# Layout of the norms' roots across partitions: matmuls become transposes, and stand a quarter of a tile earlier in three stages

## The reference

```python
for i in range(2):                      # fox mixer, then nsa mixer
    x = x + mixer_i(rmsnorm(x, norm_g[i]))
x = rmsnorm(x, final_g)
for layer in range(2):                  # hgrn mixer, then mla mixer
    x = x + mixer(_rmsnorm(x, norm_mix[layer]))
    x = x + _conv_ffn(_rmsnorm(x, norm_ffn[layer]), ...)
def _rmsnorm(x, gain):
    return x * rsqrt(mean(x * x, axis=-1) + 1e-6) * gain
def _hgrn2_mixer(h, w_in, lower_bound, out_norm, w_out):
    q, f, i, g = split(h @ w_in, 4)
    forget = lb + (1.0 - lb) * sigmoid(f)
    o = _chunk_gated_recurrence(silu(q), 1 - forget, i, log(forget))
    return (_rmsnorm(o, out_norm) * silu(g)) @ w_out   # norm per head of 128
def _conv_ffn(h, w_up, conv_w, conv_b, w_down):
    gate, up = split(causal_conv3(h @ w_up), 2)        # 2 x 2816
    return (silu(gate) * up) @ w_down
```

## Time and profile before

| | |
|---|---|
| median of 3 runs | 1025.72 us (1021.55, 1025.72, 1028.17) |
| the profiled execution | 1021.83 us |
| its span, first to last instruction | 1020.0 us |
| PE (matmul) busy | 986.8 us, 8176 records |
| DVE busy | 767.8 us |
| ACT busy | 549.8 us |
| POOL busy | 65.8 us |
| mean granted clock of TensorE | 0.996 of full speed |

### The profile page before, as it was taken

How to read it: one execution, slowest core, us unless ns; L and a number is a source line. 1 busy time by engine, 2 the same in 40 slices (tenths; PEclk the granted TensorE clock), 3 DMA queues, 4 the chain that set the end, 5 groups by cost and what they waited for, 6 DMA issues and landing times. The chain is left out here.

```text
span 1020.0 us, 20361 instructions
## 1 busy us (share of the span) xinstructions
PE 986.8 (97%) x8176; PEld 938.1 (92%) x8178; DVE 767.8 (75%) x1300; ACT 549.8 (54%) x869; POOL 65.8 (6%) x54
## 2 busy tenths in 40 slices
PE   7999999999999999999999999999999999999997
PEld 5999999897778999899999999999998899999996
DVE  5766776867787678598657978788876759888885
ACT  5545555364766656543555545454765556545541
POOL 4000004000000400000030000000000430000000
PEclk9999999999999999999999999999999999999999
DMA  8544435893112557400455766665531347765741
GB/s 281 173 130 147 137 126 150 246 287 99 63 43 84 165 172 215 152 1 16 151 166 145 216 176 195 175 201 170 151 124 42 85 124 206 207 206 170 217 149 42
DMA packets 184141, 153.08 MB, mean 150 GB/s; under 512 B 12477, under 2 KB 176900, under 8 KB 184068
## 3 DMA queue, kind: packets, MB, share of 16 engines
q1 hardware_dynamic: 183858, 152.01, 49.9%
q10 hardware_dynamic: 210, 0.05, 0.0%
HBM read 148.91 MB, written 1.05 MB: 147 GB/s over the span
## 5 line engine op out<-in xcount | busy, mean ns | idle before, releaser
L447 PE MATMUL bank<-h_high,w_high 128*128 128x256 f32 x1312 | 373.2, 284 | 8.3 <-DVE ffn_normed L1096 3.4
L448 PE MATMUL bank<-h_low,w_high 128*128 128x256 f32 x1312 | 365.7, 279 | 0.0
L449 PE MATMUL bank<-h_high,w_low 128*128 128x256 f32 x1312 | 365.6, 279 | 0.0
L399 ACT ACTIVATE w_high<-ring 128x2048 fp32r<-128x2048 f32 x137 | 261.7, 1913 | 136.8 <-PE bank L449 130.4
L409 DVE TENSOR_TENSOR w_low<-ring,w_high 128x2048 fp32r<-128x2048 f32 x118 | 271.4, 2301 | 26.9 <-ACT w_high L399 26.6
L447 PEld LDWEIGHTS bank<-h_high,w_high 128*128 128x128 f32 x1312 | 247.4, 189 | 11.2 <-issue 6.4
L448 PEld LDWEIGHTS bank<-h_low,w_high 128*128 128x128 f32 x1312 | 248.9, 190 | 0.5 <-issue 0.5
L449 PEld LDWEIGHTS bank<-h_high,w_low 128*128 128x128 f32 x1312 | 247.4, 189 | 0.0
L447 PE MATMUL bank<-ffn_hidden_high,w_high 128*128 (+1 forms) x352 | 98.2, 279 | 2.8 <-DVE ffn_hidden_low L1129 2.8
L448 PE MATMUL bank<-ffn_hidden_low,w_high 128*128 (+1 forms) x352 | 98.0, 279 | 0.0
L449 PE MATMUL bank<-ffn_hidden_high,w_low 128*128 (+1 forms) x352 | 98.0, 279 | 0.0
(11 more groups left out here) (352 smaller groups left out, 1735.1 us busy)
## 6 DMA issues: line engine op xcount, KB each, us to landing
ring<-in_ffn_w_up_dram SPq DMA_DIRECT2D x44, 1024.0 KB, 6.0
ring<-in_ffn_w_down_dram SPq DMA_DIRECT2D x22, 1024.0 KB, 5.0
ring<-in_fox_w_in_dram SPq DMA_DIRECT2D x16, 1024.0 KB, 5.9
ring<-in_hgrn_w_in_dram SPq DMA_DIRECT2D x16, 1024.0 KB, 5.6
ring<-in_nsa_w_in_dram SPq DMA_DIRECT2D x14, 1024.0 KB, 5.5
ring<-in_fox_w_out_dram SPq DMA_DIRECT2D x4, 1024.0 KB, 5.0
ring<-in_nsa_w_out_dram SPq DMA_DIRECT2D x4, 1024.0 KB, 5.0
ring<-in_hgrn_w_out_dram SPq DMA_DIRECT2D x4, 1024.0 KB, 5.0
```

The lines of the kernel that those rows point to most:

```text
L399: i = nc.scalar.activation(dst, src, ACT.Copy)
L447: nc.tensor.matmul(o, ah, bh, start=start, stop=False, **kw)
L448: nc.tensor.matmul(o, ah, bl, start=False, stop=False, **kw)
L449: return nc.tensor.matmul(o, al, bh, start=False, stop=stop, **kw)
```

## The change

`spread` lays a column out by a transpose in place of a matmul. In `ffn_pair` the norm's spread is called after the first quarter (12 matmuls) of pair 1, not after half of it. In the third mixer it is called after quarter 0 of tile `t_f + 1`, not after quarter 1. The four instructions on the lower bounds become a function that `finish` calls as its `meanwhile`, so that they stand behind the inversion of the roots and ahead of the wait for the spread.

```diff
@@ spread
-                mm = nc.tensor.matmul(o[:, i * P:(i + 1) * P], column.broadcast_to([P, P]), ident, start=True,
-                                      stop=True)
+                mm = nc.tensor.transpose(o[:, i * P:(i + 1) * P], column.broadcast_to([P, P]), ident)
@@ ffn_pair
-        def ffn_pair(pe, t, u, bank_wait, ready=None, later=0, half=None):
+        def ffn_pair(pe, t, u, bank_wait, ready=None, later=0, quarter=None):
...
-                if half and e == 0:
-                    half()
+                    if quarter and (e, c) == (0, 3):
+                        quarter()
@@ ffn
-                    ffn_pair(pe, pair_tile(1), u0 + 1, (u0 + 1) // 2, half=lambda: nrm.spread(pe))
+                    ffn_pair(pe, pair_tile(1), u0 + 1, (u0 + 1) // 2, quarter=lambda: nrm.spread(pe))
@@ third mixer, tensor
-                    by_feature(pe, t_f + i, hsp, between=lambda q, i=i: (i, q) == (1, 1) and nrm_hgrn.spread(pe))
+                    by_feature(pe, t_f + i, hsp, between=lambda q, i=i: (i, q) == (1, 0) and nrm_hgrn.spread(pe))
@@ third mixer, vector
+                def lower_bounds():
+                    dve.wait_ge(lb_exp, 1)
+                    nc.vector.reciprocal(lower_rest[:, :], lower_exp[:, :]).then_inc(lb_step, 1)
...
+                    dve.wait_ge(lb_step, 5)
+
...
-                dve.wait_ge(lb_exp, 1)
-                nc.vector.reciprocal(lower_rest[:, :], lower_exp[:, :]).then_inc(lb_step, 1)
...
-                dve.wait_ge(lb_step, 5)
-                nrm_hgrn.finish(dve)
+                nrm_hgrn.finish(dve, meanwhile=lower_bounds)
```

More of the change, by code:

```diff
@@ L2337, in evac_rows @@
                                             ALU.mult).then_inc(freed(t + i), 1)
+                def lower_bounds():
+                    dve.wait_ge(lb_exp, 1)
+                    nc.vector.reciprocal(lower_rest[:, :], lower_exp[:, :]).then_inc(lb_step, 1)
+                    dve.wait_ge(lb_step, 2)
+                    nc.vector.tensor_tensor(lower_exp[:, :], lower_exp[:, :], lower_rest[:, :], ALU.mult).then_inc(lb_step, 1)
+                    dve.wait_ge(lb_step, 3)
+                    nc.vector.tensor_tensor(lower[:, :], lower_exp[:, :], lower_exp[:, :], ALU.subtract).then_inc(lb_step, 1)
+                    dve.wait_ge(lb_step, 4)
+                    nc.vector.tensor_scalar(lower_rest[:, :], lower[:, :], -1.0, 1.0, ALU.mult, ALU.add).then_inc(lb_step, 1)
+                    dve.wait_ge(lb_step, 5)
                 def forget_gate(i):
```

## The result

The changed kernel took 1012.99 us in the median of four runs (1007.5 to 1013.61), the kernel before, beside it, 1023.63 (1015.39 to 1028.17): ratio 0.9888, interval 0.9845 to 0.9932. The forecast was 1017.3, with a range from 1012.0: the medians differ by 10.6 us, and the result lies near the quick end. The span of the profiled executions went from 1020.0 to 1011.6 us, by the 8.4 us that were forecast. That this figure is met so well is luck, as the stages show. Two later sets of runs gave ratios of 0.9963 (0.9936 to 0.9989, ten runs) and 0.9934 (0.9907 to 0.9961, twelve runs), smaller gains than the first four runs had. Over all runs of the study, those that the ratios leave out as slow among them, the mean is 1021.8 us before (72 runs, 1012.7 to 1030.2) and 1015.9 after (26 runs, 1007.5 to 1019.6): **5.9 us**, 0.6%.

What follows compares the result with a forecast made beforehand. TensorE, busy for 97% of the span, was taken as the bound. Terms of 0.4, 1.6, 1.4, 1.8 and 3.2 us sum to 8.4 us off 1025.72, giving 1017.3 us, range 1012.0 to 1023.5.

Steps and rivals of the forecast that it cites:

- Transposes: In `spread` on TensorE: one record a column in place of two, saving 0.10 us a column.
- The heads' roots of the third mixer: 16 columns in four lots between quarters of two tiles, as transposes: 1.6 us saved.
- The fourth mixer's: Head roots, 16 columns: 0.8 us from lots one and two, 0.6 from three and four, together 1.4 us.
- Third mixer: Norm's roots a quarter earlier, bounds behind the norm: PE's next tile 1.8 us sooner, bounds 1.2 to 2.1.
- Feed-forward stages: Roots behind 12 matmuls: row copy and pair 3 start 1.6 us earlier in each stage, 3.2 us in all.
- given back in `last_down`: Rival: PE waits longer at the feed-forward stages' end; 5.6 us left, 1020.1 us, or 4.2 and 1021.5; chance 0.15.
- Sum: Whole kernel: terms of 0.4, 1.6, 1.4, 1.8 and 3.2 make 8.4 us saved, giving 1017.3 us.
- 46 x 0.05: Rival that a transpose is cheaper than a record, over all columns: 2.5 us more saved, 1014.8 us; chance 0.05.
- range of 6 to 10 us: Forecast's own range of savings for the whole kernel, given as the terms' bounds: 1015.7 to 1019.7 us.
- widened by the runs' own scatter of some 3 us to either side: Step for the whole kernel's time: takes 1015.7 to 1019.7 us out to 1012.0 to 1023.5.
- The rival that it falls in the roots: Clock drops to 1.2 GHz in the roots' stretches, some 26 us at half clock: 1030.3 us; chance 0.04.
- The rival that a fall stays out: One or two clock falls fewer, by shorter stalls at 366.34 and 542 or earlier roots: 1015.6 to 1013.9 us; chance 0.12.

Runs made afterwards that it cites:

- drained: Changed kernel with a TensorE wait for its own last matmul behind each `step_down` of the loop; median 1024.9 us in ten runs.
- mixer_half: Changed kernel with the third mixer's roots behind two quarters of the tile again; 1014.8 us in one run.
- bounds_ahead: Changed kernel with the lower bounds ahead of the norm again; 1018.3 us in one run.
- transposes_only: Kernel before with transposes in `spread` and nothing moved; median 1012.5 us in four runs, ratio 0.9898.
- moves_only: Changed kernel with the matmul put back in `spread`; median 1020.5 us in ten runs, ratio 0.9963.
- behind_three: Changed kernel with the feed-forward norms' roots behind 3 matmuls of pair 1 in place of 12; median 1013.5 us in 11 runs.
- silu_quarter: Changed kernel with a one-column Silu on ACT behind its second high part, roots still behind 12 matmuls; median 1017.0 us in 11 runs.

## Why the prediction was right, and by what luck

- **Transposes.** Right in kind: one record a column in place of two. The column's saving of 0.10 us was a little small: it is (0.81 - 0.35) / 4 = 0.115. The heads' roots of the third mixer gave 1.86 us where 1.6 were said; all lots kept moving, as said of the DVE chain. The fourth mixer's, from the first lot to the last, took 10.34 us before and 8.84 after: 1.5, forecast 1.4.
- **Third mixer.** Forecast 1.8 us, measured 2.3 in the mixer's stretch. The row copy came 1.7 us earlier against the block's start (5.38 to 3.65 us, forecast 3.56), and the wait for `w_low` went as a whole. PE's next tile started 2.1 us sooner, at the quick end of what was said, since `w_low` took 2.28 us and not 3.25; the prediction had left both open. Against a `w_low` of 2.28 us in both, the stretch would have gained 2.3 - 1.0 = 1.3 us (an estimate). The DVE's wait at the copy was 1.19 us where 1.8 was said: 3.21 less the 1.7 of the copy, less the 0.3 by which the DVE, with the bounds behind the inversion, comes to it later.
- **Feed-forward stages.** Forecast 1.6 us each; start 1 against start 2 at like spacing gives 19.34 to 17.70 (quick) and 19.52 to 17.89 (slow), 1.6 both times. The wait at the copy fell from 3.54 to 1.90. The wait at pair 3 is 0.63 in place of 0.4 us, since PE is there earlier still. Nothing was given back in `last_down`: rest is within 0.2 us of 160.0 or 165.4 in all kernels but drained. The wait in `last_down` goes with the spacing, 1.63 us behind a quick stretch and 1.20 behind a slow one, before and after alike.
- **Sum.** By stages the change is worth 1.9 + 1.5 + 2.3 + 3.3 + about 0.2 = 9.2 us. The 0.2 is the first mixer's norm; the second mixer's was given back in its longer wait for `w_low`. The two profiles show 8.4, because the one after had another 3.4 us at half clock in the first mixer (+0.9 at its block's start), and their slow stages cancel. The runs' means show 5.9. Of the difference, 1.0 may be `w_low`, if most runs before had it short; the rest would mean that stages are slow more often in the changed kernel. Only profiles can show that, and they hold few stages.
- **Two slips in the working.** 46 x 0.05 is 2.3, not 2.5 (a quarter of 0.22 is 0.055, which gives 2.5). And the range of 6 to 10 us isn't that of the terms: their bounds for the two moved places alone add up to 5.0 to 9.0.
- **The step that failed** is "widened by the runs' own scatter of some 3 us to either side": I took the scatter for noise about the forecast, of no concern to the change. A large part of it is made of steps of 5.3 to 5.8 us, one for each long stretch, taken at PE's restarts, and a change that takes a restart away bears on them. With the changed kernel's own restart at pair 3 (its three profiles, mixer_half, bounds_ahead, and drained up to its first added wait) the stretch was slow in 8 of 12 stages, with a restart of another length (before, transposes_only, moves_only, behind_three, silu_quarter) in 3 of 10. So few stages can differ that much by chance. Why a restart leads to one or the other, and whether the change shifts the odds, stays open.
- **Clock.** The rival that it falls in the roots is out: stretches at 0.50 lay in the first mixer, at the third mixer's block start and in the fourth mixer's attention, never at the heads' roots. In three profiles (before, changed and mixer_half) one began 2.9 to 3.7 us behind the last of these lots, so with matmuls as with transposes. The rival that a fall stays out didn't come true either: the profile after had one such stretch more. The rule cited for the clock (the Trainium skill, TensorE: Matmul & The Clock Gate, Part 4: PE-mode transpose) found no support here: at the heads' roots (four transposes in a row) and at the sixteen (1.9 us) the clock was 1.00 in every profile. Longer runs of transposes weren't tried. The Terms of that page of the Trainium skill say "4× faster for FP32"; here transposes start 0.109 us apart and the records of a float32 matmul 0.108 to 0.112, two a column: two to one.

## What to carry to other kernels

Lay a column out by a transpose, not by a float32 matmul with the identity. When a chain moves, look for what is late next on each engine, above all for a table load that can be done in an earlier wait. Before two profiles are subtracted, compare stages that the change doesn't touch: here they differed by 5.7 us, two thirds of the gain. Look at the length of the same instruction in both, too: one `w_low` made 1.0 us of it. And where you can, take away waits ahead of a long unbroken stretch as a whole: one too short to be listed still restarts TensorE.

## What the runs showed of the hardware

At a granted clock of 1.00 and with no idle time, 128 x 128 by 128 x 256 float32r matmuls start either 0.1133 or 0.1178 us apart. In the feed-forward stages the spacing was taken at a restart behind a wait and kept for up to 170 us (1484 matmuls); in the second mixer it changed without one, where the kind of product changed. The Trainium skill (TensorE: Matmul & The Clock Gate, Back-to-back issue gap) gives N / 2.4 + 2.5 ns for a single matmul by itself, 0.109 us for 256 columns, and for streams of weight loads and matmuls 81 ns with 128 columns and 131 ns with 512. The rows show two spacings for one and the same stream, both above the first figure and between the last two. Each of the two feed-forward stages has 1392 matmuls from pair 3 to `last_down`: the 4% between the spacings, less what the wait in `last_down` gives back, is 5.3 to 5.8 us a stage, near the whole 5.9 us that the change gave in the means.

Where a POOL cast (128 x 1536) and a DVE subtraction (`w_low`, 128 x 2048) overlapped, the one that began second took longer, by most of the overlap. The subtraction took 3.25 us in place of 2.28 with 1.1 us of overlap (before); the cast took 3.52 us in place of 1.47 with 2.2 (mixer_half), and 2.38 with 1.1 (changed).
